# Two transformer blocks on one core: the second attention's per-head keys from split operands in three fp32r passes

## The chip, the core and the metric

The kernel runs on one core of one Trainium2 chip. The metric is device time in microseconds (us). A program of one core is timed as a whole; the median of three runs of the kernel before is 2732.92 us.

## The reference, cut to what matters

Two blocks run one after the other on 256 tokens of width 2048, all in float32. The second block has a gated linear recurrence, an attention with 16 heads over a latent of rank 512, a projection and a large mixture of experts. The change lies in that attention. Each head h builds its keys and values from the normed latent `c_kv` (256 tokens x 512):

```python
ckv = rmsnorm(ckv, kv_norm_g[l])
...
q_lat = jnp.einsum('bqhd,hcd->bqhc', qb, w_uk)
logits = jnp.einsum('bqhc,bqkc->bqhk', q_lat, c_sel).astype(jnp.float32) * HEAD_DIM_2 ** -0.5
...
o_lat = jnp.einsum('bqhk,bqkc->bqhc', p, c_sel)
o = jnp.einsum('bqhc,hcd->bqhd', o_lat, w_uv)
```

The kernel computes the same thing in the other order: the keys of head h are `w_uk[h]^T c_kv^T` (128 x 256, a sum over 512), and the queries meet these keys.

## The kernel before, in words

Everything that is multiplied by a large weight is done in three products of split operands. A weight unit is a tile `raw` of 128 x 1024 that SyncE loads from a stream in HBM into one of four slots. ScalarE copies it to `w_hi` in the type fp32r (L474), VectorE subtracts to get `w_lo` (L483), and TensorE multiplies `w_hi` with the high and low halves of the activations together (512 columns, L532) and `w_lo` with the high half (256 columns, L539). Two units make a pair. A slot may be overwritten by ScalarE only when TensorE has finished the unit that was in it (semaphore `unit_done`), so ScalarE's next copy starts behind TensorE's end of a unit. VectorE then adds the two halves of a result (L550).

Each engine runs its own program, and its instructions execute in the order written there. The code around the change, in the order in which it runs:

- The index scores of the attention (L1668 on VectorE) end with a causal mask added (L1685). The latent is turned into `CKVT` (four chunks of 128 x 256) by ScalarE, long before the heads.
- The recurrence, `rnn_block(j)` for j = 0 to 15. For each j TensorE multiplies two pairs (`rnn_inputs`, `rnn_queries`) with the gate products of j - 1 between them (L2346). GpSimd scales a row (L646) and stages the gate weights (L649), VectorE makes the convolution (L1729, L1733). `rnn_queries(j)` may start only when VectorE has added the halves of the one before (L550).
- The heads, `one_head(h)` for h = 0 to 15. For each h TensorE does: pair 0 (four runs of L532 and L539); the output of head h - 1 (L2395); the logits of head h (L2408); pair 1; `keys_values(h + 1)`, that is the keys (L2368) and the values (L2373) of the next head; and the transposes of the probabilities (L2419). `keys_values(0)` stands ahead of the loop.
- For one head, ScalarE (`head`) does: KTS copy (L982), the load of the next head's `UKV` (128 x 1024, keys' weights in its first half, values' weights in the second, issued at L985), two `w_hi` copies, the low half of the gate row TG (L545), in head 0 a square root over 128 x 4096 (L994), the exponentials (L997), the Tanh of TG (L1000), two `w_hi` copies (the first unit of the pair, then the second), and the rest of the head.
- VectorE (`one_head`) does: two `w_lo` units (L483), the sum of TG (L550), mask and scale of the logits (L1797), their maximum (L1801, L1803), the end of the head before (L1773 to L1782), the reciprocal and the scaling of the probabilities (L1811, L1814), the copy of the values and the scan (L1787, L1788, L1819, L1822), two `w_lo` units and the sum of TA.
- GpSimd does per head: copy of the query row (L653), scaling of TG and of TA (L657).

The keys' matmul takes plain fp32 operands: 4 matmuls of 128 x 256, each of which stands in the trace as two passes.

Of the kernel before, what the change touches and what calls it, by code (L numbers as in the profile page):

```python
# [35 lines left out]
P = 128  # L36
S = 256
# [97 lines left out]
def build(nc, stream, x, p_t, rows, consts, params, rg_w, ukv, keys_t, out):  # L135
    ctx = ExitStack()
    with ctx:
# [20 lines left out]
            pass  # L158
        gate_in_hi = gate_act[:, :, 0, :]
        gate_in_lo = gate_act[:, :, 1, :]  # L160
        big = sb("big", [P, NB * S])
        with nc.sbuf_tensor("expert_act", [P, 2, 2, S], F32R) as expert_act:
            pass
        weighted = sb("weighted", [P, 4, 2, P], F32R)
# [13 lines left out]
        def at(lo, n):  # L178
            return big[:, lo:lo + n]
# [44 lines left out]
        UKV = at(28672, 8 * P).rearrange("p (k n) -> p k n", k=8)  # L224
        CKVT = at(29696, RT * S).rearrange("p (k n) -> p k n", k=RT)
        ISC = at(30720, TT * S).rearrange("p (t n) -> p t n", t=TT)
        AMASK = at(31232, TT * S)
        KW = at(31744, TT * P).rearrange("p (t n) -> p t n", t=TT)
        KID = at(32000, TT * P).rearrange("p (t n) -> p t n", t=TT)
        KIT = at(32256, S)  # L230
# [95 lines left out]
        row_ready = sem("row_ready")  # L326
        table_ready = sem("table_ready")
        ukv_ready = sem("ukv_ready")
        xf_ready = sem("xf_ready")
        x_saved = sem("x_saved")  # L330
        out_saved = sem("out_saved")
# [35 lines left out]
        conv_b_used = sem("conv_b_used")  # L367
        staged = sem("staged")
        scored = sem("scored")
        sc_masked = sem("sc_masked")  # L370
        sc_max = sem("sc_max")
        exps = sem("exps")
        probs_turned = sem("probs_turned")
# [41 lines left out]
        v_kept = sem("v_kept")  # L415
        q_staged = sem("q_staged")
        logits_made = sem("logits_made")
        logits_masked = sem("logits_masked")
        max_ready = sem("max_ready")
        p_exp = sem("p_exp")  # L420
        p_ready = sem("p_ready")
# [202 lines left out]
        @block.gpsimd  # L624
        def _(pool):
            step = Steps(pool, g_step)
            for one in primed:
                for each in one if isinstance(one, list) else [one]:
                    pool.sem_inc(each, 1)
            pool.sem_inc(summed, SUMMED_AT_START)  # L630
            pool.sem_inc(copied, 4)
            pool.sem_inc(pool_summed, 4)

            with pool.Fori(0, TT) as t:
                with pool.Fori(0, KVH) as g:
                    u = t * KVH + g
                    pool.wait_ge(qk_kept, 12)
                    pool.wait_ge(scored, u + 1)
                    pool.tensor_copy(QST, QT[:, bass.ds(2 * g, 2), bass.ds(t * P, P)]).then_inc(staged, 1)
                    pool.tensor_copy(KST, KTP[:, bass.ds(g, 1), bass.ds(t * P, 2 * P)]  # L640
                                     .rearrange("p o n -> p (o n)")).then_inc(staged, 1)

            with pool.Fori(0, KT) as j:
                wait_summed(pool, block_of("rnn", j, 2, 0))
                pool.wait_ge(row_kept, 1)
                pool.tensor_tensor(XP[:, 3:3 + S], XP[:, 3:3 + S], RSTD_ROW, ALU.mult).then_inc(scaled, 1)  # L646
                pool.wait_ge(table_ready, 16)
                pool.wait_ge(rg_done, j + 1)
                pool.tensor_copy(WST, RGW[:, bass.ds(j, 1), :].rearrange("p o n -> p (o n)")).then_inc(w_staged, 1)  # L649
            wait_summed(pool, block_of("rnn", KT - 1, 2, 1))  # L650
            with pool.Fori(0, H2) as h:
                pool.wait_ge(logits_made, h + 1)
                pool.tensor_copy(QS2, QT2[:, bass.ds(h, 1), :].rearrange("p o n -> p (o n)")).then_inc(q_staged, 1)  # L653
                for n in range(2):
                    wait_summed(pool, block_of("heads", h, 2, n))
                    gate_rows = [TG, TA][n]
                    pool.tensor_tensor(gate_rows, gate_rows, RSTD_ROW, ALU.mult).then_inc(scaled, 1)  # L657

            def add_copied(dest, halves, block):
                pool.wait_ge(copied, block + 5)  # L660
                pool.tensor_tensor(dest, halves[:, 0:S], halves[:, S:2 * S], ALU.add).then_inc(pool_summed, 1)

            with pool.Fori(0, PH) as h:
                for a in range(2):
                    pool.wait_ge(ps_made[a], h + 1)
                    add_copied(PQS[:, a, :], QUERY_HALVES[:, a, :], h * 4 + a)
                for n in range(2):
                    add_copied(Z_HALVES[:, n, 0:S], Z_HALVES[:, n, :], h * 4 + (2 + n))
            pool.wait_ge(slots_kept, 3)

            with pool.Fori(0, S // 8) as i:
                pool.wait_ge(hot2, i * 8 + 1)
                pool.tensor_copy(idx8, second_index[:, bass.ds(i * 8, 8)]).then_inc(g_step, 1)
                pool.wait_ge(g_step, i + 1)
                for s in range(8):
                    pool.wait_ge(hot_used[s % 4], i * 2 + s // 4 + 1)
                    pool.sem_inc(hot_turn, 1)
                    pool.tensor_scalar(hot[:, s % 4, :], iota, idx8[:, s:s + 1], None, ALU.is_equal)\  # L678
                        .then_inc(hot2, 1)

            pool.wait_ge(row_ready, 48)
            for t in range(TT):
                pool.wait_ge(y_added, 4 * t + 2)
                pool.tensor_tensor(OUT[:, t, 0:1024], XF[:, t, 0:1024], final_row[:, 0:1024], ALU.mult)\  # L684
                    .then_inc(gained, 1)
# [3 lines left out]
        def _(act):  # L689
# [230 lines left out]
            for k in range(RT):  # L920
                act.wait_ge(ckv_turned, 2 * (k // 2) + 2)
                act.activation(CKVT[:, k, :], banks[6 + k // 2][:, (k % 2) * S:(k % 2 + 1) * S], ACT.Copy,
                               scale=pa("kv_gain")[:, k:k + 1]).then_inc(ckvt_kept, 1)
            act.dma_start(UKV, ukv[0:1, :, :].rearrange("o p (k n) -> p (o k) n", n=P)).then_inc(ukv_ready, 16)

            with act.Fori(0, IH // 4 - 1) as i:
                for n in range(2):
# [35 lines left out]
                low_half(act, QT2[:, bass.ds(j, 1), :].rearrange("p o n -> p (o n)"), banks[1])  # L963

            rnn_block(0, first=True)
            with act.Fori(1, KT) as j:
                rnn_block(j)
            rnn_gates(KT - 1)
            rnn_decay(KT - 1)

# [8 lines left out]
            def head(h, first=False, last=False):  # L979
                act.wait_ge(k_made, h + 1)  # L980
                act.wait_ge(logits_made, h + 1)
                act.activation(KTS, banks[2][:, 0:S], ACT.Copy).then_inc(k_kept, 1)  # L982
                if not last:
                    act.wait_ge(v_made, h + 1)
                    act.dma_start(UKV, ukv[bass.ds(h + 1, 1), :, :].rearrange("o p (k n) -> p (o k) n", n=P))\  # L985
                       .then_inc(ukv_ready, 16)
                ahead(split_hi, act, "heads", h, 2, 0)
                act.wait_ge(unit_done, 2 * pair_of("heads", h, 2, 0) + 2)
                act.wait_ge(gr_used, h + 1)
                low_half(act, TG, banks[0])  # L990
                if first:

                    act.wait_ge(rw_ready, 1)
                    act.activation(RW, RW, ACT.Sqrt, scale=0.25).then_inc(rw_root, 1)  # L994
                act.wait_ge(max_ready, h + 1)
                for t in range(TT):
                    act.activation(LG[:, t, :], LG[:, t, :], ACT.Exp, bias=nm[:, t:t + 1],  # L997
                                   accum_out=esum[:, t:t + 1]).then_inc(p_exp, 1)
                act.wait_ge(scaled, H2 + h * 2 + 1)
                act.activation(TG, TG, ACT.Tanh, scale=0.5).then_inc(gr_tanh, 1)  # L1000
                ahead(split_hi, act, "heads", h, 2, 1)
                act.wait_ge(unit_done, 2 * pair_of("heads", h, 2, 1) + 2)
                act.wait_ge(head_mixed, h + 1)
                low_half(act, TA, banks[1])
                if last:
                    keep_probs(h)
                act.wait_ge(scaled, H2 + h * 2 + 2)
                act.activation(TA, TA, ACT.Tanh, scale=0.5).then_inc(ga_tanh, 1)
                if not last:
                    keep_probs(h)  # L1010
# [238 lines left out]
        def _(dve):  # L1249
# [432 lines left out]


            for t in range(TT):
                step(dve.tensor_tensor(IWORK[:, t, :], ISC[:, t, :], c("causal")[:, t * S:(t + 1) * S], ALU.add))  # L1685

            def next_eight():
                for t in range(TT):
# [428 lines left out]
        def _(pe):  # L2117
# [244 lines left out]

            def keys_values(h):
                pe.wait_ge(ukv_ready, h * 16 + 16)
                pe.wait_ge(ckvt_kept, RT)
                pe.wait_ge(k_kept, h + 1)
                for k in range(RT):
                    ins = pe.matmul(banks[2][:, 0:S], UKV[:, k, :], CKVT[:, k, :], start=(k == 0), stop=(k == RT - 1))  # L2368
                ins.then_inc(k_made, 1)
                pe.wait_ge(v_kept, h + 1)  # L2370
                for st in range(2):
                    for k in range(RT):
                        ins = pe.matmul(banks[3][:, st * P:(st + 1) * P], CKVT[:, k, st * P:(st + 1) * P],  # L2373
                                        UKV[:, RT + k, :], start=(k == 0), stop=(k == RT - 1))
                ins.then_inc(v_made, 1)
# [345 lines left out]
```

## Time and profile before

| | |
|---|---|
| median of 3 runs | 2732.92 us (2732.72 to 2734.38) |
| span of the profiled execution | 2730.6 us; its own time is not listed apart from the span |
| TensorE busy | 2707.6 us, 99% of the span |
| VectorE, ScalarE, GpSimd busy | 69%, 51%, 13% |
| the stretch of the heads | about 812 to 1083 us |
| keys of the heads, L2368 | 30.3 us busy |
| granted TensorE clock, mean | 0.999 |

The span counts from the first to the last instruction. In the timeline a row gives the start in us from the span's start, the duration in us, the engine, the line and operation, the names of the tiles and how many instructions are merged. A matmul's duration overlaps with the next one's, so that the distance of starts, not the duration, is what one matmul costs. PEld rows are TensorE's weight loads.

### The profile page before, as it was taken

How to read it: one execution, taken by the hardware profiler on the slowest of the kernel's cores; microseconds unless marked ns; L12 is line 12 of the kernel's file. 1: busy time of each engine (PE TensorE's matmuls, PEld its weight loads, DVE VectorE, ACT ScalarE, POOL GpSimd, SP SyncE). 2: the span in 40 equal slices, each digit the busy share in tenths (PEclk: the TensorE clock that was granted, in tenths of full speed). 3: DMA queues.
4: the chain of work that ended last, by engine and by line, in shares of the span. 5: the costliest groups of instructions: out<-in, count | busy, mean ns of one | idle time of the engine just before them, and what ended most of it. 6: DMA issues, size and time to landing. Idle time of an engine off the chain costs nothing.

```text
span 2730.6 us, 48285 instructions
## 1 busy us (share of the span) xinstructions
PE 2707.6 (99%) x14430; PEld 2332.0 (85%) x14430; DVE 1890.1 (69%) x3047; ACT 1391.3 (51%) x2118; POOL 358.1 (13%) x422
## 2 busy tenths in 40 slices
PE   8999999999999999999999999999999999999998
PEld 7888888898888888888888888888888888888887
DVE  6666665668986666479997888886665555555555
ACT  6455445556665444465455555554544444444444
POOL 0000000000001111011104666660000000000000
PEclk9999999999999999999999999999999999999999
DMA  6544455454554444555565555556666666655564
GB/s 256 192 155 160 148 196 184 176 215 162 172 176 159 155 159 140 200 193 195 196 199 202 197 190 197 194 196 206 211 215 217 218 213 218 212 194 192 194 239 156
DMA packets 162487, 522.17 MB, mean 191 GB/s; under 512 B 18048, under 2 KB 42880, under 8 KB 161408
## 3 DMA queue, kind: packets, MB, share of 16 engines
q1 hardware_dynamic: 131472, 478.35, 51.0%
q10 hardware_dynamic: 30960, 43.14, 4.5%
q8 instruction: 29, 0.48, 0.1%
q14 instruction: 26, 0.21, 0.0%
HBM read 504.63 MB, written 16.78 MB: 191 GB/s over the span
## 4 chain that ended last, share of the span: by engine, by line
PE 94%; DVE 3%; ACT 1%; issue 1%; DMA 0%; SPq 0%; ACTq 0%; DVEq 0%
PE bank L532 31%; PE bank L539 16%; PE bank L2571 8%; PE bank L2573 8%; PE bank L2572 8%; PE bank L572 4%; PE bank L574 4%; PE bank L573 4%; PE bank L2540 1%; PE bank L2373 1%; PE bank L2368 1%; DVE w_lo L483 1%; PE bank L506 1%; PE bank L507 1%; PE bank L508 1%
## 5 line engine op out<-in xcount | busy, mean ns | idle before, releaser
L483 DVE TENSOR_TENSOR w_lo<-raw,w_hi 128x1024 fp32r<-128x1024 f32 x902 | 1095.0, 1224 | 694.7 <-ACT w_hi L474 683.4
L474 ACT ACTIVATE w_hi<-raw 128x1024 fp32r<-128x1024 f32 x902 | 952.1, 1060 | 943.1 <-PE bank L539 359.8
L532 PE MATMUL bank<-act,w_hi 128*128 128x512 f32 x3840 | 975.8, 396 | 2.3 <-DVE big L1420 1.1
L532 PEld LDWEIGHTS bank<-act,w_hi 128*128 128x128 f32 x3840 | 692.6, 189 | 133.7 <-issue 7.2
L539 PEld LDWEIGHTS bank<-act,w_lo 128*128 128x128 f32 x3840 | 520.0, 191 | 33.1
L539 PE MATMUL bank<-act,w_lo 128*128 128x256 f32 x3840 | 535.8, 282 | 0.0
L2571 PE MATMUL bank<-w_hi,expert_act 128*128 128x512 f32 x1008 | 392.6, 389 | 0.1
L2573 PE MATMUL bank<-w_hi,expert_act 128*128 128x512 f32 x1008 | 392.5, 389 | 0.0
L2572 PE MATMUL bank<-w_lo,expert_act 128*128 128x512 f32 x1008 | 392.4, 389 | 0.0
L678 POOL TENSOR_SCALAR hot<-cst,stat 128x128 fp32r<-128x128 f32 x256 | 255.1, 1011 | 129.1 <-PE bank L2540 128.7
L2571 PEld LDWEIGHTS bank<-w_hi,expert_act 128*128 128x128 f32 x1008 | 189.3, 188 | 39.5 <-DVE cst L550 0.5
L2573 PEld LDWEIGHTS bank<-w_hi,expert_act 128*128 128x128 f32 x1008 | 189.3, 188 | 39.2
L2572 PEld LDWEIGHTS bank<-w_lo,expert_act 128*128 128x128 f32 x1008 | 189.3, 188 | 39.1
L572 PE MATMUL bank<-w_hi,act 128*128 128x512 f32 x320 | 126.0, 394 | 1.5 <-DVE w_lo L483 0.8
L574 PE MATMUL bank<-w_hi,act 128*128 128x512 f32 x320 | 124.8, 390 | 0.0
L573 PE MATMUL bank<-w_lo,act 128*128 128x512 f32 x320 | 124.6, 389 | 0.0
L684 POOL TENSOR_TENSOR big<-big 128x1024 f32<-128x1024 f32 x2 | 5.8, 2878 | 874.9 <-DVE big L2078 874.9
L2005 DVE SCALAR_TENSOR_TENSOR weighted<-cst,slot_t 128x256 fp32r<-128x256 f32 x256 | 116.0, 511 | 0.0
L646 POOL TENSOR_TENSOR big<-big 128x256 f32<-128x256 f32 x16 | 11.1, 696 | 485.0 <-DVE big L550 485.0
L572 PEld LDWEIGHTS bank<-w_hi,act 128*128 128x128 f32 x320 | 60.1, 188 | 15.7 <-DVE w_lo L483 1.3
L574 PEld LDWEIGHTS bank<-w_hi,act 128*128 128x128 f32 x320 | 60.1, 188 | 12.6
L573 PEld LDWEIGHTS bank<-w_lo,act 128*128 128x128 f32 x320 | 60.1, 188 | 12.1
(332 smaller groups left out, 2518.1 us busy)
## 6 DMA issues: line engine op xcount, KB each, us to landing
raw<-in_stream SPq DMA_DIRECT2D x902, 512.0 KB, 3.7
z_kept<-cst ACTq DMA_DIRECT2D x96, 128.0 KB, 2.1
cst<-z_kept ACTq DMA_DIRECT2D x96, 128.0 KB, 4.0
big<-in_ukv ACTq DMA_DIRECT2D x16, 512.0 KB, 4.6
big<-in_rows ACTq DMA_DIRECT2D x3, 1024.0 KB, 5.5
big<-in_x SPq DMA_DIRECT2D x2, 1024.0 KB, 9.7
big<-in_rg_w ACTq DMA_DIRECT2D x1, 2048.0 KB, 11.2
x_kept<-big ACTq DMA_DIRECT2D x1, 2048.0 KB, 8.3
```

What stands on the lines that cost most here:

```text
L474: act.activation(w_hi[:, s, :], raw[:, s, :], ACT.Copy).then_inc(hi_ready, 1)
L483: dve.tensor_tensor(w_lo[:, s, :], raw[:, s, :], w_hi[:, s, :].bitcast(F32), ALU.subtract).then_inc(lo_ready, 1)
L532: pe.matmul(bank[:, :], w_hi[:, s, kk * P:(kk + 1) * P], act2[:, k, :, :].rearrange("p a n -> p (a n)"), start=(k == 0), stop=False)
L539: mm = pe.matmul(bank[:, 0:S], w_lo[:, s, kk * P:(kk + 1) * P], act_hi[:, k, :], start=False, stop=(k == KT - 1))
L572: pe.matmul(outs[t], a_hi, hi, start=(k == 0), stop=False)
L573: pe.matmul(outs[t], a_hi, lo, start=False, stop=False)
L574: mm = pe.matmul(outs[t], a_lo, hi, start=False, stop=(k == KT - 1))
L678: pool.tensor_scalar(hot[:, s % 4, :], iota, idx8[:, s:s + 1], None, ALU.is_equal)\
L2005: dve.scalar_tensor_tensor(out=weighted[:, s, :, :], in0=iota.unsqueeze(1).broadcast_to([P, 2, P]), scalar=first_index[:, bass.ds(tok, 1)] ...
L2571: pe.matmul(o, a_hi, hi, start=first, stop=False, skip_group_check=True)
L2572: pe.matmul(o, a_hi, lo, start=False, stop=False, skip_group_check=True)
L2573: mm = pe.matmul(o, a_lo, hi, start=False, stop=False, skip_group_check=True)
```

## The change

The keys of each head come from three fp32r products per chunk. ScalarE makes `ckvt_hi` once (one Copy of 128 x 1024 behind the making of `CKVT`) and `uk_hi` for each head (a Copy of 128 x 512). GpSimd makes `ckvt_lo` once (a subtraction of 128 x 1024, ahead of its recurrence loop) and `uk_lo` for each head (a subtraction of 128 x 512). TensorE waits for all of them before the keys. `uk_hi` of head h + 1 stands on ScalarE behind the Tanh of TG of head h and ahead of the two `w_hi` copies; `uk_lo` of head h + 1 stands on GpSimd behind its scaling of TG of head h. For head 0 the high part is made ahead of the last `rnn_block` and the low part behind GpSimd's recurrence loop. The last passes of two loops are written out for this. `ckvt_lo` lies where the index scores were, so GpSimd waits for the two masked sums (L1685), which count on `rel_used` now, and the mask `AMASK` is moved to another place. Two semaphores that nothing used are gone.

```diff
+        with nc.sbuf_tensor("below_uk", [P, 11008], F32), \
+                nc.sbuf_tensor("uk_hi", [P, RT, P], F32R) as uk_hi, \
+                nc.sbuf_tensor("uk_lo", [P, RT, P], F32R) as uk_lo:
+            pass
...
-        AMASK = at(31232, TT * S)
+        AMASK = at(32000, TT * S)
...
+            def split_uk_lo(h):
+                pool.wait_ge(uk_hi_ready, h + 1)
+                pool.tensor_tensor(uk_lo[:, :, :], UKV[:, 0:RT, :], uk_hi[:, :, :].bitcast(F32), ALU.subtract)\
+                    .then_inc(key_lo_ready, 1)
+
+            pool.wait_ge(ckvt_kept, RT + 1)
+            pool.wait_ge(rel_used, 2 * IH + TT + 1)
+            pool.tensor_tensor(ckvt_lo[:, :, :], CKVT, ckvt_hi[:, :, :].bitcast(F32), ALU.subtract)\
+                .then_inc(key_lo_ready, 1)
             with pool.Fori(0, KT) as j:
...
+            split_uk_lo(0)
             wait_summed(pool, block_of("rnn", KT - 1, 2, 1))
-            with pool.Fori(0, H2) as h:
+
+            def scale_head(h, last=False):
                 pool.wait_ge(logits_made, h + 1)
                 pool.tensor_copy(QS2, QT2[:, bass.ds(h, 1), :].rearrange("p o n -> p (o n)")).then_inc(q_staged, 1)
                 for n in range(2):
                     wait_summed(pool, block_of("heads", h, 2, n))
                     gate_rows = [TG, TA][n]
                     pool.tensor_tensor(gate_rows, gate_rows, RSTD_ROW, ALU.mult).then_inc(scaled, 1)
+                    if not n and not last:
+                        split_uk_lo(h + 1)
...
             act.dma_start(UKV, ukv[0:1, :, :].rearrange("o p (k n) -> p (o k) n", n=P)).then_inc(ukv_ready, 16)
+            act.wait_ge(ckvt_kept, RT)
+            act.activation(ckvt_hi[:, :, :], CKVT, ACT.Copy).then_inc(ckvt_kept, 1)
+
+            def split_uk_hi(h):
+                act.wait_ge(ukv_ready, h * 16 + 16)
+                act.wait_ge(k_made, h)
+                act.activation(uk_hi[:, :, :], UKV[:, 0:RT, :], ACT.Copy).then_inc(uk_hi_ready, 1)
...
             rnn_block(0, first=True)
-            with act.Fori(1, KT) as j:
+            with act.Fori(1, KT - 1) as j:
                 rnn_block(j)
+            act.wait_ge(ukv_ready, 16)
+            act.wait_ge(w_staged, KT - 1)
+            act.activation(uk_hi[:, :, :], UKV[:, 0:RT, :], ACT.Copy).then_inc(uk_hi_ready, 1)
+            rnn_block(KT - 1)
...
                 act.activation(TG, TG, ACT.Tanh, scale=0.5).then_inc(gr_tanh, 1)
+                if not last:
+                    split_uk_hi(h + 1)
                 ahead(split_hi, act, "heads", h, 2, 1)
...
-                step(dve.tensor_tensor(IWORK[:, t, :], ISC[:, t, :], c("causal")[:, t * S:(t + 1) * S], ALU.add))
+                dve.tensor_tensor(IWORK[:, t, :], ISC[:, t, :], c("causal")[:, t * S:(t + 1) * S], ALU.add)\
+                   .then_inc(rel_used, 1)
+            dve.wait_ge(rel_used, 2 * IH + TT + 1)
...
             def keys_values(h):
                 pe.wait_ge(ukv_ready, h * 16 + 16)
-                pe.wait_ge(ckvt_kept, RT)
+                pe.wait_ge(ckvt_kept, RT + 1)
+                pe.wait_ge(key_lo_ready, h + 2)
                 pe.wait_ge(k_kept, h + 1)
                 for k in range(RT):
-                    ins = pe.matmul(banks[2][:, 0:S], UKV[:, k, :], CKVT[:, k, :], start=(k == 0), stop=(k == RT - 1))
+                    pe.matmul(banks[2][:, 0:S], uk_hi[:, k, :], ckvt_hi[:, k, :], start=(k == 0), stop=False)
+                    pe.matmul(banks[2][:, 0:S], uk_hi[:, k, :], ckvt_lo[:, k, :], start=False, stop=False)
+                    ins = pe.matmul(banks[2][:, 0:S], uk_lo[:, k, :], ckvt_hi[:, k, :], start=False, stop=(k == RT - 1))
                 ins.then_inc(k_made, 1)
```

## Rows read from the trace of the kernel before

**Rows 1.** The page's busy times of each engine, with share and instruction count.

```profile
PE 2707.6 (99%) x14430; PEld 2332.0 (85%) x14430; DVE 1890.1 (69%) x3047; ACT 1391.3 (51%) x2118; POOL 358.1 (13%) x422
```

**Rows 2.** Stretch of one head: length, busy us of PE, PEld, DVE, ACT, POOL, clock, DMA.

```profile
863.18:880.05 16.87, 16.87 (x103) 15.10 (x101) 11.06 (x22) 7.25 (x14) 1.81 (x3) 1.00 0.48 155
```

**Rows 3.** Timeline, TensorE, from one head's keys to the next head's.

```profile
863.18 1.89 PE L2368 MATMUL bank<-big 128*128 128x256 f32 x8
...
864.91 1.95 PE L2373 MATMUL bank<-big 128*128 128x128 f32 x16
...
871.78 1.12 PE L539 MATMUL bank<-act,w_lo 128*128 128x256 f32 x8
...
872.73 1.03 PE L2395 MATMUL bank<-big 128*128 128x256 f32 x4
...
880.05 1.89 PE L2368 MATMUL bank<-big 128*128 128x256 f32 x8
```

**Rows 4.** The same timeline, ScalarE and VectorE, between pair 0 and the keys.

```profile
872.93 1.06 ACT L474 ACTIVATE w_hi<-raw 128x1024 fp32r<-128x1024 f32 x1 [1.73 <-PE bank L539]
...
874.11 1.23 DVE L483 TENSOR_TENSOR w_lo<-raw,w_hi 128x1024 fp32r<-128x1024 f32 x1 [1.56 <-ACT w_hi L474]
...
877.41 0.51 ACT L997 ACTIVATE big<-big,stat 128x256 f32<-128x256 f32 x1 [3.15 <-DVE stat L1803]
...
878.41 0.40 ACT L1000 ACTIVATE big<-big 128x256 f32<-128x256 f32 x1
...
878.71 1.04 ACT L474 ACTIVATE w_hi<-raw 128x1024 fp32r<-128x1024 f32 x1
...
879.39 0.62 DVE L1814 TENSOR_SCALAR big<-big,stat 128x256 f32<-128x256 f32 x2
```

**Rows 5.** Groups by line (ScalarE L862), then single lines of GpSimd: min/median/max ns.

```profile
L862 ACT ACTIVATE big<-big 128x512 f32<-128x512 f32 x4 | 2.5, 632 | 10.3 <-DVE big L1600 10.2
...
L646 POOL TENSOR_TENSOR big<-big x16: 635/638/1552, 631.1 to 807.8; 128x256 f32<-128x256 f32 x16
...
L684 POOL TENSOR_TENSOR big<-big x2: 2405/2878/3351, 2715.9 to 2721.0; 128x1024 f32<-128x1024 f32 x2
...
L678 POOL TENSOR_SCALAR hot<-cst,stat x256: 601/843/1647, 1449.1 to 1842.1; 128x128 fp32r<-128x128 f32 x128
```

**Rows 6.** Timeline, head 0, where ScalarE has the square root too.

```profile
829.30 1.89 PE L2368 MATMUL bank<-big 128*128 128x256 f32 x8
...
831.92 0.40 ACT L1000 ACTIVATE big<-big 128x256 f32<-128x256 f32 x1
...
832.77 0.68 DVE L1819 TENSOR_TENSOR_SCAN big<-big 128x256 f32<-128x256 f32 x1
832.91 0.42 PEld L2419 LDWEIGHTS bank<-cst,big 128*128 128x128 f32 x4
```

**Rows 7.** Timeline, start of the recurrence: GpSimd, VectorE, TensorE.

```profile
631.14 1.55 POOL L646 TENSOR_TENSOR big<-big 128x256 f32<-128x256 f32 x1 [324.25 <-DVE big L550]
...
632.73 0.46 DVE L1729 TENSOR_SCALAR big<-big,par 128x256 f32<-128x256 f32 x1 [0.53 <-POOL big L646]
...
636.93 0.41 DVE L550 TENSOR_TENSOR big<-big,bank 128x256 f32<-128x256 f32 x1
...
638.24 2.21 PE L532 MATMUL bank<-act,w_hi 128*128 128x512 f32 x8
```

**Rows 8.** Timeline, end of the recurrence: GpSimd's last staging, the keys of head 0.

```profile
808.34 0.40 POOL L649 COPY big<-big 128x256 f32 x1
...
812.87 1.89 PE L2368 MATMUL bank<-big 128*128 128x256 f32 x8
```

**Rows 9.** Timeline, TensorE, its first matmuls and where they get faster.

```profile
7.20 0.77 PE L2152 MATMUL bank<-w_hi,act 128*128 128x512 f32 x1 [7.20 <-DVE w_lo L483]
...
12.45 0.63 PE L2152 MATMUL bank<-w_hi,act 128*128 128x512 f32 x1
...
13.70 0.40 PE L2153 MATMUL bank<-w_lo,act 128*128 128x512 f32 x1
```

More of the change, by code:

```diff
@@ L160, in build @@
         gate_in_lo = gate_act[:, :, 1, :]
+        with nc.sbuf_tensor("below_uk", [P, 11008], F32), \
+                nc.sbuf_tensor("uk_hi", [P, RT, P], F32R) as uk_hi, \
+                nc.sbuf_tensor("uk_lo", [P, RT, P], F32R) as uk_lo:
+            pass
+        with nc.sbuf_tensor("below_ckvt_lo", [P, 30720], F32), \
+                nc.sbuf_tensor("ckvt_lo", [P, RT, S], F32R) as ckvt_lo:
+            pass
         big = sb("big", [P, NB * S])
+        with nc.sbuf_tensor("ckvt_hi", [P, RT, S], F32R) as ckvt_hi:
+            pass
         with nc.sbuf_tensor("expert_act", [P, 2, 2, S], F32R) as expert_act:
@@ L328, in build @@
         ukv_ready = sem("ukv_ready")
+        uk_hi_ready = sem("uk_hi_ready")
+        key_lo_ready = sem("key_lo_ready")
         xf_ready = sem("xf_ready")
@@ L369, in build @@
         scored = sem("scored")
-        sc_masked = sem("sc_masked")
         sc_max = sem("sc_max")
@@ L417, in build @@
         logits_made = sem("logits_made")
-        logits_masked = sem("logits_masked")
         max_ready = sem("max_ready")
@@ L657, in _ @@
                     pool.tensor_tensor(gate_rows, gate_rows, RSTD_ROW, ALU.mult).then_inc(scaled, 1)
+                    if not n and not last:
+                        split_uk_lo(h + 1)
+            with pool.Fori(0, H2 - 1) as h:
+                scale_head(h)
+            scale_head(H2 - 1, last=True)
             def add_copied(dest, halves, block):
```

## The prediction

> **What bounds the kernel now.** I read the page's busy times first: TensorE is busy for 2707.6 us of the span, the others far less [rows 1]. So work taken from TensorE is worth its full time, and work given to ScalarE or GpSimd costs nothing, but only as long as TensorE never waits for it. The second view is the stretch of one head: 16.87 us, TensorE busy for all of it at full clock, ScalarE 7.25, GpSimd 1.81 [rows 2]. The engines that get the new work are mostly idle. That says nothing of when they are idle, so the third view is TensorE's timeline in one head. Keys start at 863.18, values at 864.91, the head's first pair ends about where L2395 starts, 872.73, and the next keys start at 880.05 [rows 3]. The fourth is the chain on ScalarE and VectorE between that 872.73 and the 880.05, since the change hangs a new piece on its end [rows 4].
>
> **TensorE's gain.** The keys take 864.91 - 863.18 = 1.73 us for four plain fp32 matmuls (eight passes). The replacement is 12 fp32r matmuls of 128 x 256. The nearest row is L539, fp32r of the same width with a new weight tile each: eight in 872.73 - 871.78 = 0.95 us, 0.119 each [rows 3]. Twelve cost 1.43 us, so a head gains **0.30 us**, 16 heads 4.8 us. The bounds are small, since the row is the same kind: at 0.13 each the gain is 0.17. By the Trainium skill (TensorE: Matmul & The Clock Gate, section "Back-to-back issue gap") a matmul of 256 columns at full clock takes N/2.4 + 2.5 = 109 ns, an estimate by which the gain would be 0.42; the trace has 119, and the measurement decides.
>
> **The new wait, steady heads.** `keys_values(h + 1)` now waits for GpSimd's `uk_lo`, which waits for ScalarE's `uk_hi`, which stands behind the Tanh of TG of head h. When is that? ScalarE's second `w_hi` copy waits for TensorE to end the first pair and starts at 872.93, 0.20 behind it; VectorE's `w_lo` follows at 874.11, then the sum of TG, mask and maximum, then the exponentials at 877.41, the Tanh at 878.41, and ScalarE's next instruction at 878.71 [rows 4]. Each starts when the one before is done, so the chain is tied to TensorE's own 872.73: if TensorE comes later, so does it. `uk_hi` takes that 878.71. A ScalarE pass of 128 x 512 takes 632 ns [rows 5], so it ends at 879.34. GpSimd starts about 0.06 later. It did its TG scaling before 877 and has nothing else. Its subtraction of 128 x 512 is not in the trace. A clean two-input one of 256 elements takes 635 ns and one of 1024 takes 2405 [rows 5], so (2405 - 635) / 768 = 2.30 ns an element and 635 + 256 x 2.30 = 1.225 us. That gives 880.63, and with 0.1 us of handover TensorE can start at 880.73, where before it started at 880.05: 0.68 of waiting.
>
> Part of that price is unsure. VectorE scales the probabilities from 879.39, just when GpSimd starts [rows 4], and the row of L646 shows what an overlap can do: 1552 ns at worst against 638 in the median [rows 5]. The Trainium skill (SBUF — State Buffer, section "Who interferes with whom") says that VectorE in a 2-port mode, or with two SBUF inputs, and GpSimd exclude each other for a whole instruction, and that the first to issue wins. What each order would give I take from the rows. If VectorE is first, GpSimd loses up to the 0.62 of L1814 and the wait is 1.3; if GpSimd is first, the wait stays 0.68, and VectorE's L1814 comes 1.2 us later, at 880.6, which hurts nobody, as the transposes that need it start behind keys and values, not before 884. I take half, 0.3: a wait of 1.0. Net per head 1.0 - 0.30 = **+0.70 us**, bounds +0.38 and +1.0. Heads 1 to 14 make these keys: 14 x 0.70 = +9.8 (5.3 to 14).
>
> The wait doesn't grow from head to head, because the part from keys to the end of the next first pair shrinks by 0.30 and the rest is this chain. The new period is about 16.87 + 0.70 = 17.57. Behind `uk_hi` on ScalarE stand the two `w_hi` copies of the next head's second pair, 0.63 later; TensorE needs them half a head later. Behind `uk_lo` on GpSimd stands TA's scaling, whose input comes behind that. The load of the weights of the next head is issued as before, some 9 us ahead of the Tanh. Nothing of these reaches TensorE.
>
> **Head 0** is another case. ScalarE has the square root first, and the Tanh of TG comes at 831.92, when the keys of head 1 had already started at 829.30 [rows 6]. `uk_hi` would run from 832.22 to 832.85, GpSimd from 832.91, and in its way is the scan at 832.77 with two SBUF inputs, for 0.68 [rows 6]. The subtraction ends at 834.15 to 834.7, TensorE starts at 834.25 to 834.8: a wait of 4.95 to 5.5. Keys and values used to end just at the transposes (832.91), with at most 0.1 to win back there. Net of 0.30 and 0.1: **+4.6 to +5.1**, I take 4.8.
>
> After so long a pause TensorE's clock is a question. The only case in the trace is the start: idle for 7.2 us, then 13 matmuls of 512 columns with starts (12.45 - 7.20) / 12 = 0.44 apart and 0.63 long, and by 13.70 they are 0.40 long, though the profile grants full clock there too [rows 9]. I read the first as the 1.2 GHz level, for some 5.7 us, of which half, 2.8 us, is lost. The pause here is shorter than 7.2, and others of up to a few tenths show nothing. I take 0 and keep +2.8 as the bound.
>
> **Start of the recurrence.** GpSimd now subtracts 128 x 1024 (2.40 clean) behind the masked scores at about 630.6, ahead of its first row scaling, which was at 631.14 and released VectorE's L1729 at 632.73 [rows 7]. It would end at 633.0; VectorE's `w_lo` in between, with two SBUF inputs, is held up or holds it up; then the row scaling, and L1729 at about 634.9, 2.2 late. VectorE's later work shifts with it: the sum L550 at 636.93 becomes 639.1, and `rnn_queries(1)` on TensorE, before at 638.24, waits for it [rows 7]. Cost **+1.3 us** once, bounds 0 and 2. The Copy of `ckvt_hi` on ScalarE (some 1.06, as L474) comes while TensorE has a whole pair of work; zero, and at most its 1.06 if that cover is gone.
>
> **Keys of head 0.** `uk_hi` is made a block ahead. `uk_lo` starts behind the last staging (808.34 + 0.40) and takes 1.23 to 2, done by 810.8, 2 us ahead of 812.87 [rows 8]. No wait: the gain of **-0.3** stays. The order of instructions in two peeled loops, the moved mask and the counted sums cost nothing: their engines wait there already.
>
> **The sum**: -0.3 + 1.3 + 4.8 + 9.8 = **+15.6 us**. The profiled span of 2730.6 becomes 2746.2. The median of the runs is 2.3 above that span and I carry the 2.3 over: 2732.9 + 15.6 = **2748.5 us** (+0.57%).
>
> **Rivals.** (1) *The wait isn't there in the steady heads.* The point is 0.68 us: if the new pieces come that much sooner against TensorE than I read, the heads 1 to 14 gain 0.30 each, with head 0 and the recurrence still paying: 2732.9 - 0.3 x 15 + 4.8 + 1.3 = 2734.5, and 2728.1 if those are covered too (16 x 0.30). For it: ScalarE has 9.6 us to spare in a head. Against: every start in the chain stands in the rows, and it has no gap that could close. Chance 0.09, both ends inside 0.2% of the time before (5.5 us, about what a measurement of this kernel can tell from no change), bar noise. (2) *GpSimd is slow at writing fp32r.* Its one instruction with an fp32r output takes 601 ns at best for 128 elements [rows 5], 4.7 ns an element, double the 2.30. Then a subtraction takes 2.4, not 1.23, each steady head pays 1.2 more: 14 x 1.2 + 1.2 + about 2 = 20 us on top, 2768. For it: the type. Against: L678 is a compare with a scalar from SBUF, another operation, and the two-input row is the nearer one. Chance 0.10. (3) *The clock falls after head 0's pause*: 2751.3, within my own range, chance 0.3 inside the forecast. (4) *The change doesn't do what it says*: the fp32r products could cost more than L539. At the 0.216 of one fp32 pass twelve take 2.6 and not 1.43: 2748.5 + 16 x 1.17 = 2767. L539 is the same type and width, so 0.03.
>
> **How the numbers follow.** Forecast 0.78 (2742.4 to 2756.5 by its bounds: 5.3 + 4.6 - 0.3 + 0, and 14 + 5.1 + 2 + 2.8 - 0.3), rival 1 0.09, rivals 2 and 4 0.13. The range is the forecast's with a little of the slow side: 2740 to 2760. Slower by over 0.2% (above 2738.4): 0.78 + 0.13, less a few chances that half of the wait is missing: 0.89. Within: 0.09. Faster: 0.02.
>
> **What would show it.** In the changed profile: L2368's successors with starts 0.119 apart, 1.43 per head; an idle time of TensorE of about 1.0 us ahead of each head's keys, released by GpSimd's `uk_lo`, and 5 us in head 1's; a period of 17.6; `uk_lo` at 1.2 to 1.6 us on GpSimd; one TensorE wait of about 1.3 near 640. The prediction is wrong if TensorE's idle time ahead of the keys is under 0.3 us, if GpSimd's subtraction takes over 2 us, or if the clock falls in the heads.

## The result, and the profile after

| | median, us | to the kernel before |
|---|---|---|
| before | 2732.8 | |
| changed kernel | 2748.7 (2747.6 to 2749.1) | 1.0057, interval 1.0043 to 1.0071 |

The change makes the kernel slower by 15.9 us; the prediction was 2748.5. The profiled span went from 2730.6 to 2746.7 us. In the changed kernel the lines are renumbered: the keys are L2410 to L2412, the values L2417, the transposes L2463, `uk_hi` L957, `uk_lo` L654, `ckvt_lo` L659, the Tanh L1037, GpSimd's row scaling L664, and L532, L539, L2395 and L2408 are now L541, L548, L2439 and L2452.

First the stretch of one steady head, to be set beside [rows 2]. The columns are length, busy us of PE, PEld, DVE, ACT and POOL, the granted clock and the DMA share:

```profile
873.28:890.65 17.37, 16.83 (x105) 15.06 (x105) 12.16 (x22) 7.74 (x16) 3.10 (x4) 1.00 0.48 152
```

A head takes 17.37 us, not 16.87, and TensorE is no longer busy for all of it. What it waits for says the list of waits (us in total, times, longest):

```profile
PE bank L2410 <- POOL uk_lo L654: 13.1, 15, 5.5
```

Fifteen waits, one for each head that has a next one. TensorE's timeline in head 0 and the two heads behind it, as [rows 3] and [rows 6] before:

```profile
829.55 1.11 PE L548 MATMUL bank<-act,w_lo 128*128 128x256 f32 x8
836.21 0.55 PE L2410 MATMUL bank<-ckvt_hi,uk_hi 128*128 128x256 f32 x1 [5.55 <-POOL uk_lo L654]
836.56 0.41 PE L2411 MATMUL bank<-ckvt_lo,uk_hi 128*128 128x256 f32 x1
...
838.91 3.12 PE L2417 MATMUL bank<-big 128*128 128x128 f32 x16
841.87 0.60 PE L2463 MATMUL bank<-cst,big 128*128 128x128 f32 x4
...
855.91 0.39 PE L2410 MATMUL bank<-ckvt_hi,uk_hi 128*128 128x256 f32 x1 [0.54 <-POOL uk_lo L654]
...
871.63 1.11 PE L548 MATMUL bank<-act,w_lo 128*128 128x256 f32 x8
873.28 0.39 PE L2410 MATMUL bank<-ckvt_hi,uk_hi 128*128 128x256 f32 x1 [0.54 <-POOL uk_lo L654]
873.50 0.28 PE L2411 MATMUL bank<-ckvt_lo,uk_hi 128*128 128x256 f32 x1
...
874.81 1.95 PE L2417 MATMUL bank<-big 128*128 128x128 f32 x16
...
1081.78 0.38 PE L2410 MATMUL bank<-ckvt_hi,uk_hi 128*128 128x256 f32 x1 [0.55 <-POOL uk_lo L654]
```

The steady head: the pair's last eight L548 start at 871.63 and cost 0.95, so keys could start at 872.58 and start at 873.28, 0.70 late. The keys take 874.81 - 873.28 = 1.53 us for 1.73 before: twelve starts 0.12 apart, but the first, behind the pause, is followed after 0.22. So 0.70 of wait less 0.20 of gain is +0.50. (The 0.54 in brackets is shorter than 0.70 because it counts from 872.74, where the duration of the last L548 ends.) And the chain that ends the wait, on the three other engines in that head, as [rows 4]:

```profile
870.95 0.40 ACT L1037 ACTIVATE big<-big 128x256 f32<-128x256 f32 x1
871.25 0.62 ACT L957 ACTIVATE uk_hi<-big 128x512 fp32r<-128x512 f32 x1
...
871.95 1.28 POOL L654 TENSOR_TENSOR uk_lo<-big,uk_hi 128x512 fp32r<-128x512 f32 x1 [2.93 <-ACT uk_hi L957]
...
871.93 1.71 DVE L1855 TENSOR_SCALAR big<-big,stat 128x256 f32<-128x256 f32 x2
```

Tanh, `uk_hi`, `uk_lo`, keys, with no gap of more than 0.1 us. The contended neighbour is VectorE: its L1855 (L1814 in [rows 4]) took 0.62 before and takes 1.71, until 873.64, behind the end of GpSimd's instruction at 873.23. The row merges two instructions: the first takes 1.45 us and the second 0.34. GpSimd wasn't slowed: its 1.28 is what it takes alone (1.29, in the run `once` below). That is what the Trainium skill says of the shared port pair (SBUF — State Buffer, section "Who interferes with whom"): one of the two waits for the other's whole instruction. Here the row of L654 shows who won in the steady heads. By the starts in the trace VectorE's instruction came first, by 0.02 us, and it was the one held up; at that distance the starts don't tell the winner.

The start of the recurrence, as [rows 7]:

```profile
630.85 2.41 POOL L659 TENSOR_TENSOR ckvt_lo<-big,ckvt_hi 128x1024 fp32r<-128x1024 f32 x1 [323.87 <-DVE big L1724]
633.21 1.63 POOL L664 TENSOR_TENSOR big<-big 128x256 f32<-128x256 f32 x1
...
631.20 3.14 DVE L492 TENSOR_TENSOR w_lo<-raw,w_hi 128x1024 fp32r<-128x1024 f32 x1
634.88 0.45 DVE L1770 TENSOR_SCALAR big<-big,par 128x256 f32<-128x256 f32 x1 [0.53 <-POOL big L664]
...
639.63 2.12 PE L541 MATMUL bank<-act,w_hi 128*128 128x512 f32 x8 [0.93 <-DVE big L559]
```

VectorE's `w_lo` (1.23 alone) takes 3.14, since GpSimd holds it up; then it holds up GpSimd's row scaling, 1.63 for 0.64. VectorE's convolution starts at 634.88 and not at 632.73, and `rnn_queries(1)` at 639.63 and not at 638.24.

TensorE's granted clock around head 0, in which TensorE stood still from 830.7 to 836.2 (the clock is the figure behind POOL's):

```profile
829.00:850.00 21.00, 15.45 (x86) 14.23 (x85) 8.17 (x14) 11.04 (x17) 2.68 (x3) 0.84 0.38 116
```

After that pause the key matmuls start 0.21 apart and not 0.12 (838.91 - 836.21 = 2.70 us for the keys, 2.96 for the values): that is the 1.2 GHz level.

Where the 16.1 us of the span come from, read from TensorE's starts in both kernels. The column "later" is how much later the row of after starts than its counterpart of before:

| place | before | after | later | step |
|---|---|---|---|---|
| `rnn_queries(1)` | 638.24 | 639.63 | +1.39 | +1.4 start of the recurrence |
| keys of head 0 | 812.87 | 814.16 | +1.29 | -0.1 |
| keys of head 1 could start | 829.30 | 830.50 | +1.20 | -0.3 keys of head 0, +0.2 its first logits |
| transposes of head 0 | 832.91 | 841.87 | +8.96 | **+7.8** head 0 |
| keys of head 2 | 846.32 | 855.91 | +9.59 | +0.6 |
| keys of head 3 | 863.18 | 873.28 | +10.10 | +0.5 |
| keys of head 15 | 1065.6 | 1081.8 | +16.2 | **+6.1**, twelve heads by 0.50 |
| span | 2730.6 | 2746.7 | +16.1 | |

### The profile page after: what moved, and what is told of

The parts are those of the page before. It is cut to its first block, busy times and chain, and to the rows that moved or that the text cites. A ratio compares the mean times of both kernels' runs of the same rounds, so it can differ in the third digit from the quotient of the medians.

```text
span 2746.7 us, 48474 instructions
## 1 busy us (share of the span) xinstructions
PE 2709.0 (99%) x14494; PEld 2331.9 (85%) x14494; DVE 1907.8 (69%) x3047; ACT 1399.5 (51%) x2134; POOL 381.5 (14%) x439
## 4 chain that ended last, share of the span: by engine, by line
PE 85%; issue 9%; DVE 3%; POOL 1%; ACT 1%; DMA 0%; POOLq 0%; SPq 0%; DVEq 0%; ACTq 0%
PE bank L541 27%; PE bank L548 14%; PE bank L2615 8%; PE bank L2617 8%; PE bank L2616 8%; PE bank L581 4%; PE bank L583 4%; PE bank L582 4%; PE bank L2584 1%; DVE w_lo L492 1%; POOL uk_lo L654 1%; PE bank L515 1%; PE bank L516 1%; PE bank L517 1%; PE bank L2281 1%
## 5 line engine op out<-in xcount | busy, mean ns | idle before, releaser
L541 PE MATMUL bank<-act,w_hi 128*128 128x512 f32 x3840 | 975.5, 396 | 3.4 <-DVE big L1459 1.1
L541 PEld LDWEIGHTS bank<-act,w_hi 128*128 128x128 f32 x3840 | 692.0, 189 | 135.7 <-issue 8.7
L548 PEld LDWEIGHTS bank<-act,w_lo 128*128 128x128 f32 x3840 | 519.7, 190 | 33.2
L548 PE MATMUL bank<-act,w_lo 128*128 128x256 f32 x3840 | 535.5, 282 | 0.0
L581 PEld LDWEIGHTS bank<-w_hi,act 128*128 128x128 f32 x320 | 60.1, 188 | 16.1 <-DVE w_lo L492 1.3
L1184 ACT ACTIVATE big<-bank 128x256 f32 (+1 forms) x128 | 44.1, 402 | 50.8 <-PE bank L2584 50.8
```

The source lines that it names most:

```text
L541: pe.matmul(bank[:, :], w_hi[:, s, kk * P:(kk + 1) * P], act2[:, k, :, :].rearrange("p a n -> p (a n)"), start=(k == 0), stop=False)
L548: mm = pe.matmul(bank[:, 0:S], w_lo[:, s, kk * P:(kk + 1) * P], act_hi[:, k, :], start=False, stop=(k == KT - 1))
L581: pe.matmul(outs[t], a_hi, hi, start=(k == 0), stop=False)
```

## The experiments

All are made from the changed kernel unless said otherwise. Ratios are to the kernel before. W is the theory that the loss is TensorE waiting for the split. `...` marks what is left out of a diff.

**1. The per-head splits left out** (`once`).

```diff
-                if not last:
-                    split_uk_hi(h + 1)
...
-                    if not n and not last:
-                        split_uk_lo(h + 1)
...
-                pe.wait_ge(key_lo_ready, h + 2)
+                pe.wait_ge(key_lo_ready, 2)
```

> Made from the changed kernel: the key weights are split once, for head 0, and all 16 heads take their keys from that split; the splits of heads 1 to 15 are left out. The three fp32r products of each head stay. Theory W (the loss is TensorE waiting for the split, the products gain 0.30 us a head): 2732.8 - 16 x 0.30 + 1.3 (start of the recurrence) + 0.2 = 2729.5 us, no idle time ahead of the keys. Rival P (the three products themselves are dearer than the trace of before let one expect, or the peeled loops and the moved mask cost): at or above 2732.8. Rival C (contention: the wait is a side effect of ScalarE and GpSimd being fuller): 2729.5 too, and told from W by the next runs.

Measured: 2730.2 us, ratio 0.9991 (0.9982 to 1.0001), span 2729.8. The interval still holds 1, so the median alone doesn't show that the products gain. The stretch of a steady head does, to be set beside [rows 2]:

```profile
849.45:866.03 16.58, 16.58 (x107) 15.00 (x106) 11.51 (x24) 7.40 (x15) 1.81 (x3) 1.00 0.49 158
```

A head takes 16.58 us for 16.87, and TensorE doesn't wait. The three products gain 0.29, and the loss is in the splits of the heads. Rival P is out.

**2. Splits kept, plain fp32 keys** (`plain`).

```diff
-                    pe.matmul(banks[2][:, 0:S], uk_hi[:, k, :], ckvt_hi[:, k, :], start=(k == 0), stop=False)
...
+                    ins = pe.matmul(banks[2][:, 0:S], UKV[:, k, :], CKVT[:, k, :], start=(k == 0), stop=(k == RT - 1))
```

> Made from the changed kernel: all splits and waits stay, but the keys are multiplied in plain fp32 as before the change. Theory W: the waits stay and the gain of 0.30 us in each of 16 heads is lost, with about 0.3 more in head 0, where the clock is at its lower level: 2748.7 + 5.1 = 2753.8 us. Rival P: below 2748.7.

Measured: 2753.2 us, ratio 1.0076 (1.0059 to 1.0092). The gain of the products is 4.5 us in the medians, the one that the forecast had priced at 4.8. A steady head of this kernel on TensorE:

```profile
873.10 1.99 PE L2410 MATMUL bank<-big 128*128 128x256 f32 x8 [0.55 <-POOL uk_lo L654]
874.93 1.95 PE L2415 MATMUL bank<-big 128*128 128x128 f32 x16
...
890.75 1.99 PE L2410 MATMUL bank<-big 128*128 128x256 f32 x8 [0.55 <-POOL uk_lo L654]
```

The same wait, keys of 1.83 us and a head of 17.65: 1.83 - 1.53 = 0.30 is the gain of the products, behind a pause as well.

**3. TensorE waits for the low part behind the eight products with the high part** (`late_lo`).

```diff
-                pe.wait_ge(key_lo_ready, h + 2)
+                pe.wait_ge(uk_hi_ready, h + 1)
+                pe.wait_ge(key_lo_ready, 1)
...
+                pe.wait_ge(key_lo_ready, h + 2)
+                for k in range(RT):
                     ins = pe.matmul(banks[2][:, 0:S], uk_lo[:, k, :], ckvt_hi[:, k, :], start=False, stop=(k == RT - 1))
```

> Made from the changed kernel: TensorE does the eight products with the high part of the key weights first and waits for GpSimd's low part only behind them; the same work on all engines. Theory W: in heads 1 to 14 the high part is ready 0.7 us ahead of TensorE and eight products take 0.96, the low part comes 0.65 behind, so no wait is left: 14 x 0.8 = 11.2 us less; in head 0 some 1.7 less, as TensorE still waits 3.9 us there. 2735.8 us, and 2733.4 if the clock stays up in head 0. Rival C: the engines are as full as ever, so the wait comes back elsewhere: 2745 or more.

Measured: 2737.2 us, ratio 1.0017 (1.0007 to 1.0027), 11.5 less than the changed kernel. No engine does less work, so contention (rival C) is out. What is left is head 0 and the start of the recurrence: its only wait in the heads is 3.8 us, ahead of head 1's keys. It is 1.4 above the theory: in its trace the keys of steady heads start 16.71 us apart (854.36 and 871.07), 0.13 more than in `once`; why, no run shows.

**4. The high part ahead of the exponentials** (`early_hi`).

```diff
+                if not last:
+                    split_uk_hi(h + 1)
                 act.wait_ge(max_ready, h + 1)
...
                 act.activation(TG, TG, ACT.Tanh, scale=0.5).then_inc(gr_tanh, 1)
-                if not last:
-                    split_uk_hi(h + 1)
```

> Made from the changed kernel: ScalarE splits the high part ahead of the exponentials (in head 0 behind the square root) and not behind the Tanh. Theory W: ScalarE is idle for 3 us there; no wait in heads 1 to 14, 11.2 us less; in head 0 TensorE waits about 2.6 us and not 5.7, and if a pause of 2.6 leaves the clock up, another 2.4 less: 2732.0 us (2734.4 if the clock falls all the same). Rival C: 2745 or more, or the exponentials come later by the 0.6 us and the transposes wait for them: 2741.

Measured: 2733.4 us, ratio 1.0002 (0.9993 to 1.0012). In the steady heads nothing is left of the wait. Head 0 lies between the two cases that were expected:

```profile
832.40 0.36 PE L2410 MATMUL bank<-ckvt_hi,uk_hi 128*128 128x256 f32 x1 [2.53 <-POOL uk_lo L654]
...
833.07 0.28 PE L2412 MATMUL bank<-ckvt_hi,uk_lo 128*128 128x256 f32 x1
...
833.52 0.41 PE L2412 MATMUL bank<-ckvt_hi,uk_lo 128*128 128x256 f32 x1
...
834.37 3.06 PE L2417 MATMUL bank<-big 128*128 128x128 f32 x16
837.27 0.60 PE L2463 MATMUL bank<-cst,big 128*128 128x128 f32 x4
```

After a pause of 2.5 us the first products come at full rate, and from 833.3 on they take 0.41 and not 0.28: the clock falls after the pause. Keys and values take 4.87 us (837.27 - 832.40), some 1.6 more than the 3.29 at full clock in run 7.

**5. `ckvt_lo` ahead of GpSimd's last recurrence pass** (`late_ckvt`).

```diff
-            pool.tensor_tensor(ckvt_lo[:, :, :], CKVT, ckvt_hi[:, :, :].bitcast(F32), ALU.subtract)\
-                .then_inc(key_lo_ready, 1)
-            with pool.Fori(0, KT) as j:
+            with pool.Fori(0, KT - 1) as j:
+                scale_and_stage(j)
+            pool.tensor_tensor(ckvt_lo[:, :, :], CKVT, ckvt_hi[:, :, :].bitcast(F32), ALU.subtract)\
+                .then_inc(key_lo_ready, 1)
+            scale_and_stage(KT - 1)
```

> Made from the changed kernel: GpSimd makes the low part of the latent ahead of its last pass of the recurrence and not ahead of the first. Theory W: the one wait of TensorE of 0.9 us ahead of the second rnn_queries goes, 1.3 us less: 2747.4 us, the heads as before. If the start of the recurrence isn't where the 1.3 us come from: 2748.7.

Measured: 2746.9 us, ratio 1.0052 (1.0036 to 1.0067). The medians can't settle 1.3 us; the trace does:

```profile
637.68 1.03 PE L2391 MATMUL bank<-big 128*128 128x256 f32 x4
638.36 2.21 PE L541 MATMUL bank<-act,w_hi 128*128 128x512 f32 x8
```

The wait is gone, 638.36 for 639.63. Keys of head 0 start 1.2 earlier (812.97). The span is 1.7 smaller, as in head 0 the clock comes back earlier: the values there take 2.16 us from start to start (838.06 to 840.22) for 2.96.

**6. GpSimd subtracts twice** (`twice`), and TensorE waits for the second.

```diff
+                for n in range(2):
+                    pool.wait_ge(key_lo_ready, 2 * h + (1 + n))
+                    pool.tensor_tensor(uk_lo[:, :, :], UKV[:, 0:RT, :], uk_hi[:, :, :].bitcast(F32), ALU.subtract)\
+                        .then_inc(key_lo_ready, 1)
...
-                pe.wait_ge(key_lo_ready, h + 2)
+                pe.wait_ge(key_lo_ready, h * 2 + 3)
```

> Made from the changed kernel: GpSimd does each subtraction of the key weights twice. Theory W (GpSimd's time is on TensorE's path in full): 15 heads x 1.3 = 19.5 us more: 2768.2 us. If part of it is hidden (rival: the wait is ended by something else, such as ScalarE's or VectorE's work): under 2758.

Measured: 2793.0 us, ratio 1.022 (1.0204 to 1.0235), 25 us above what W gave. One head on TensorE, and the stretch of the heads (PEclk is the figure behind POOL's):

```profile
877.57 1.11 PE L548 MATMUL bank<-act,w_lo 128*128 128x256 f32 x8
880.75 0.39 PE L2412 MATMUL bank<-ckvt_hi,uk_hi 128*128 128x256 f32 x1 [2.07 <-POOL uk_lo L656]
...
881.92 0.28 PE L2412 MATMUL bank<-ckvt_hi,uk_hi 128*128 128x256 f32 x1
...
882.41 3.43 PE L2419 MATMUL bank<-big 128*128 128x128 f32 x16
```

```profile
850.00:1100.00 250.00, 225.16 (x1272) 203.45 (x1271) 157.27 (x257) 95.44 (x182) 53.79 (x61) 0.92 0.40 128
```

The period is 20.5 us, 3.15 more than in the changed kernel. The two subtractions take 2.73, 1.45 more than one, and start keys about that much later. Nearly all of the other 1.7 is the values, which take 3.27 us from start to start for 1.79 (durations 3.43 and 1.95): the granted clock is 0.92 over the stretch, and 1.00 in the changed kernel. Its pauses are nearly four times as long as those of the changed kernel, 2.07 for 0.54.

**7. Head 0's wait filled** (`filler`) and **8. the doubled wait filled** (`twice_fill`, made from 6, with 8 matmuls in every head).

The diff is that of 7:

```diff
+                if first:
+                    pe.wait_ge(ckvt_kept, RT + 1)
+                    for m in range(20):
+                        pe.matmul(banks[7][:, :], ckvt_hi[:, m % 2, 0:P],
+                                  ckvt_hi[:, 2:4, :].rearrange("p a n -> p (a n)"), start=True, stop=True)
                 if not last:
                     keys_values(h + 1)
```

> Made from the changed kernel: in head 0 TensorE does 20 matmuls of 512 columns into a bank that nothing reads, in the time in which it would wait for the low part. Theory: the clock fell because TensorE was idle for 5.6 us; with the filler (4.8 us) it stays at the 2.4 GHz level, the keys of head 1 start at the same 836.2 but take 1.43 and not 2.70 us, the values 1.79 and not 2.96: 2.4 us less, 2746.3 us. Rival: the matmuls of that stretch are slow for another reason: 2748.7, and the filler is slow as well.

> Made from the kernel in which GpSimd subtracts twice (twice): TensorE does 8 matmuls of 512 columns (1.9 us) into a bank that nothing reads ahead of each head's keys, inside its wait of 2.1 to 2.2 us. Theory (the 24 us by which twice missed its expectation are the clock, which falls in each head's pause of 2.1 us): the clock stays up in heads 1 to 14, a head costs 1.44 more than in the changed kernel and not 3.15: 2748.7 + 14 x 1.44 + 1.3 = 2770.2 us. Rival (the second subtraction holds something else up): near 2793.

Measured: 2746.6 us for the first (1.0052, 1.0036 to 1.0067). Its trace:

```profile
830.73 4.72 PE L2460 MATMUL bank<-ckvt_hi 128*128 128x512 f32 x20
836.42 0.36 PE L2410 MATMUL bank<-ckvt_hi,uk_hi 128*128 128x256 f32 x1 [0.96 <-POOL uk_lo L654]
...
837.93 1.95 PE L2417 MATMUL bank<-big 128*128 128x128 f32 x16
839.71 0.60 PE L2468 MATMUL bank<-cst,big 128*128 128x128 f32 x4
```

```profile
829.00:850.00 21.00, 20.04 (x119) 17.52 (x118) 10.53 (x18) 11.28 (x17) 3.42 (x4) 1.00 0.41 131
```

Keys and values take 839.71 - 836.42 = 3.29 us, against 841.87 - 836.21 = 5.66 in the changed kernel, and the granted clock is 1.00 where it was 0.84: 2.4 us of head 0 are the clock alone. The filler starts the keys 0.2 us later, and its median is 2.1 under the changed kernel's. The intervals of the two overlap, so that more work in a wait makes the kernel faster is shown by the trace here, and by the medians in the next run. `twice_fill` takes 2775.1 us (1.0156, 1.0141 to 1.0172), 18 us less than `twice` with more work to do:

```profile
850.00:1100.00 250.00, 246.36 (x1477) 216.59 (x1476) 171.82 (x281) 101.13 (x198) 59.41 (x66) 1.00 0.42 139
```

The clock is at 1.00 in the stretch. Of the 5 us above the expectation 1.9 are a filler in head 15, which has no wait, and 2.1 a period of 18.96 (keys at 876.94 and 895.90) and not 18.81; the rest isn't accounted for. So the rival, that the second subtraction holds something else up, falls: it is on TensorE's path with its full time, and the rest of the loss of 6 was the clock.

**9. VectorE subtracts** (`dve_lo`).

```diff
                     step(dve.reciprocal(rec[:, 0:2], esum[:, 0:2]))
+                    if not last:
+                        dve.wait_ge(uk_hi_ready, h + 2)
+                        dve.tensor_tensor(uk_lo[:, :, :], UKV[:, 0:RT, :], uk_hi[:, :, :].bitcast(F32),
+                                          ALU.subtract).then_inc(key_lo_ready, 1)
                     step.wait()
```

> Made from the changed kernel: in each head VectorE, ahead of scaling the probabilities, and not GpSimd does the subtraction for the low part of the key weights (head 0's stays on GpSimd). Theory W: it takes about 0.65 us and not 1.28, the wait of 0.7 us shrinks to 0.1, 0.6 less in 14 heads and 1.2 less in head 0: 2739.1 us. Rival: VectorE's later work is late by 0.65 and TensorE waits for that: 2748.

Measured: 2738.2 us, ratio 1.002 (1.0011 to 1.0029), 0.9 under what W gave; the rival (2748) is out. In the steady heads the list of waits has none ahead of the keys. VectorE is busier than GpSimd and takes 692 ns where GpSimd takes 1288:

```profile
L1853 DVE TENSOR_TENSOR uk_lo<-big,uk_hi x15: 691/692/693, 834.6 to 1070.7; 128x512 fp32r<-128x512 f32 x15
```

The Trainium skill (GPSIMD Engine Reference, section "Engine selection") has VectorE about twice as fast for two inputs; the ratio here is 1.86.

**10. A version meant to have no waits** (`best`: 4 and 5, with the weights of head 1 loaded ahead of the last gates and their high part split ahead of the square root) and **11. the same with that split between the last gates and decay** (`best2`, whose diff is shown; `best` lacks the line `split_uk_hi(1)`).

```diff
+            act.wait_ge(v_made, 1)
+            act.dma_start(UKV, ukv[1:2, :, :].rearrange("o p (k n) -> p (o k) n", n=P)).then_inc(ukv_ready, 16)
             rnn_gates(KT - 1)
+            split_uk_hi(1)
             rnn_decay(KT - 1)
```

> Made from the changed kernel: the high part ahead of the exponentials, the low part of the latent ahead of GpSimd's last pass of the recurrence, and for head 0 the weights of head 1 loaded ahead of the last gates and their high part split ahead of the square root. Theory W: no wait is left and 16 x 0.30 us are gained: 2728.0 us, ratio 0.9982 to the kernel before. If head 0 keeps a wait of 1 us, 2729.

> Made from the version without waits (best): the high part of head 1's key weights is split between the gates and the decay of the last recurrence block, where ScalarE is idle for 2.1 us, and no longer between the gate row's low half and the square root. Theory W: the 0.74 us for which TensorE still waited ahead of head 0's transposes goes, and with it perhaps the 0.2 us behind the first logits: 2729.2 - 0.8 = 2728.4 us. If the split holds up the decay there, the gain is given back: 2729.2.

Measured: 2729.2 us (0.9987, 0.9978 to 0.9996) and 2728.8 us (0.9986, 0.9977 to 0.9995), spans 2727.6 and 2725.9. Both beat the kernel before, by 0.13 and 0.14%, with both intervals under 1; the medians don't tell the two apart. In `best2` TensorE has one small wait left in the heads:

```profile
829.81 1.95 PE L2421 MATMUL bank<-big 128*128 128x128 f32 x16
832.18 0.66 PE L2467 MATMUL bank<-cst,big 128*128 128x128 f32 x4 [0.41 <-DVE big L1859]
```

Head 0's exponentials stand behind the square root, and with the keys 0.3 us faster the transposes come to wait for them. It was 0.74 in `best`, where the split delayed them too. The span of `best2` is 4.7 us under that of the kernel before, of the 4.8 that 16 x 0.30 promise, but its profiled run was the fastest of its eleven; the medians say 4.0.

## Why the prediction was right, point by point

- **TensorE's gain**, 0.30 a head: right. The starts are 0.12 apart, `plain` shows 0.30 and a steady head of `once` 0.29. The estimate by the rule of the Trainium skill (TensorE: Matmul & The Clock Gate, section "Back-to-back issue gap"), 0.42, doesn't hold for these matmuls.
- **The steady heads**, +0.70 each: the mechanism is right (late_lo and early_hi take it away, twice adds to it), the size was off: +0.50. The step that failed is the half of the overlap with VectorE, 0.3: the bound "GpSimd is first" was the true one, and 0.68 of wait was forecast for it, 0.70 measured. VectorE's scaling of the probabilities was held up in GpSimd's place and hurt nobody, as forecast: it ends at 873.64, and the transposes start at 876.60. Not forecast at all was the first product behind a pause, 0.10 dearer.
- **Head 0**, +4.8: its wait was forecast as 4.95 to 5.5 and is 5.7 (836.21 against 830.50); ScalarE's chain there was later by 1.39 and TensorE only by 1.2, GpSimd's pass took 1.62 beside VectorE's scan, and TensorE started 0.28 behind its end (834.31 + 1.62 = 835.93). The larger miss is the clock: I took 0 and kept 2.8 as the bound; it is 2.4 (filler). Rival 3 came true, and so did the prediction's own sign of being wrong, a clock that falls in the heads, though in head 0 alone. The 0 had no ground in the rows: the longest pauses of the kernel before, behind its start, were 1.2 us, at a clock of 1.00, and say nothing of one of 5.7. Head 0 is +7.8.
- **Start of the recurrence**, +1.3: right, 1.39 and the path as described; late_ckvt takes it away. **Keys of head 0**, no wait: right.
- The sum is right to 0.2 us in the medians (0.5 in the spans) by luck, because two misses cancel: by the table 14 heads cost 7.2 us and not 9.8, 2.6 less, and head 0 cost 7.8 and not 4.8, 3.0 more. The single number deserves less credit than the mechanism.
- **Rivals**: (1) the wait is there; (2) GpSimd writes fp32r at 1.28 us for 512 elements, 0.06 over the 1.225 interpolated from fp32 rows, and 2.41 for 1024, as in fp32; (4) out by `once` and `plain`.

## What to carry to other kernels

An engine that is idle for half of the time covers new work only if it is idle ahead of the need. Follow the last instruction in front of the new one back to the bound engine: here the whole chain was released by TensorE's own progress and left 1.34 us (878.71 to 880.05) for 1.9 us of new work, while the same ScalarE had 3 us free just ahead of the exponentials. Moving one line there turned a loss of 0.6% into none (1.0002, 0.9993 to 1.0012), and three more moves made it a gain of 0.14%. Order the consumer too: what doesn't need the late operand goes first.

## What the runs showed that was not expected

- The clock also falls after stops much shorter than head 0's 5.55 us. With a pause of 0.54 us in each head it stays at 1.00; with 2.07 in each it is at 0.92 over the heads, and each head pays 1.7 us more. There the matmuls right behind the pause are at full rate, and those about 1.4 us later at the 1.2 GHz level; in `early_hi`, after 2.53, it was 0.9 us later. A wait of 2 us thus costs nearly twice its length, and matmuls that nothing reads, put in the wait, win that back.
- Where GpSimd and VectorE collide and one clearly starts first, the price falls on whoever comes second, also when that is the engine on the path: GpSimd's row scaling took 1.63 for 0.64 us behind VectorE, VectorE's `w_lo` 3.14 for 1.23 behind GpSimd. Between two that start 0.02 us apart, as L654 and L1855 do, the later one by the trace, GpSimd's, went ahead in the steady heads; what decides that wasn't tried.
